# Moving operands of the FFN layers of a float32 block, moved to other byte offsets within 64

## What is computed

```python
D_MODEL, SEQ, D_FF = 1024, 256, 2816

def swiglu(x, w_gate, w_up, w_down):
    return (jax.nn.silu(x @ w_gate) * (x @ w_up)) @ w_down

# first block (c gives shifts, scales and gates g1, g2, g3)
h = h + 0.5 * g1 * swiglu(modulate(rmsnorm(h, norm_ff1), sh1, sc1), ...)   # FFN 0
h = h + g2 * token_mixing(modulate(rmsnorm(h, norm_mix), sh2, sc2), ...)   # mixer 0
h = h + 0.5 * g3 * swiglu(modulate(rmsnorm(h, norm_ff2), sh3, sc3), ...)   # FFN 1
h = rmsnorm(h, norm_final)
# second block
for l in range(2):
    x = x + 0.5 * swiglu_2(rms_norm(x, ffn1_norm[l]), ...)                 # FFN 2, 4
    x = x + mixers(rms_norm(x, mix_norm[l]) @ w_mix_in[l]) @ w_mix_out[l]  # mixers 1, 2
    x = x + 0.5 * swiglu_2(rms_norm(x, ffn2_norm[l]), ...)                 # FFN 3, 5
```

## Time and profile before

| what | us |
|---|---|
| median of 3 runs | 1628.17 |
| lowest, highest | 1627.67, 1628.93 |
| the profiled execution | 1633.48 |
| its span, first to last instruction | 1631.8 |
| TensorE with a matmul in flight | 1607.6 |
| VectorE busy | 1150.1 |
| ScalarE busy | 801.8 |

### The profile page before, as it was taken

The page is one execution under the profiler, slowest core; times in us unless marked ns, Lnnn a source line. Parts: engine busy times, 40 slices in busy tenths (PEclk is TensorE's granted clock), DMA queues, the critical chain, the costliest instruction groups (busy, mean ns, idle before and its releaser), DMA issues.

```text
span 1631.8 us, 33722 instructions
## 1 busy us (share of the span) xinstructions
PE 1607.6 (99%) x13569; PEld 1569.1 (96%) x13569; DVE 1150.1 (70%) x1470; ACT 801.8 (49%) x973; POOL 172.8 (11%) x193
## 2 busy tenths in 40 slices
PE   7999999999999999999999999999999999999999
PEld 4999998999999999999999999999999999999999
DVE  6877778878866657666688776656666588776653
ACT  3544445354544445444565654445444466564442
POOL 1100113700000000000043200000000025200000
PEclk9999998999999999999999999999999999999999
DMA  9998896755766477665754466558664764456653
GB/s 333 309 316 251 245 317 205 231 175 163 206 181 181 136 199 207 186 182 158 222 155 130 131 181 190 164 170 224 186 192 139 203 196 138 135 157 190 179 160 115
DMA packets 501553, 315.62 MB, mean 193 GB/s; under 512 B 14815, under 2 KB 489674, under 8 KB 501450
## 3 DMA queue, kind: packets, MB, share of 16 engines
q1 hardware_dynamic: 491824, 282.33, 60.7%
q0 software_dynamic: 8496, 29.92, 5.3%
q10 hardware_dynamic: 1130, 1.90, 0.3%
HBM read 313.04 MB, written 1.05 MB: 192 GB/s over the span
## 4 chain that ended last, share of the span: by engine, by line
PE 72%; DVE 3%; ACT 1%; issue 0%; ACTq 0%; DVEq 0%
PE accs L1755 20%; PE accs L1757 19%; PE accs L1756 19%; PE wide L1793 1%; PE accs L1793 1%; PE wide L1795 1%; PE accs L1795 1%; PE wide L1794 1%; PE accs L1794 1%; DVE wlo L1065 1%; PE wide L2026 1%; PE accs L1853 1%; PE accs L1854 1%; PE accs L1855 1%; PE bank L2097 0%
## 5 line engine op out<-in xcount | busy, mean ns | idle before, releaser
L1755 PE MATMUL accs<-uhi_room,whi 128*128 128x256 f32 x2304 | 650.8, 282 | 3.1 <-DVE ulo L1116 1.2
L1757 PE MATMUL accs<-uhi_room,wlo 128*128 128x256 f32 x2304 | 644.6, 280 | 0.0
L1756 PE MATMUL accs<-ulo,whi 128*128 128x256 f32 x2304 | 644.3, 280 | 0.0
L754 ACT CAST whi<-raw 128x2048 fp32r<-128x2048 f32 (+2 forms) x294 | 499.9, 1703 | 107.2 <-PE accs L1757 61.8
L1065 DVE TENSOR_TENSOR wlo<-raw,whi 128x2048 fp32r<-128x2048 f32 (+2 forms) x249 | 496.3, 2001 | 4.1 <-ACT gat L992 3.1
L1755 PEld LDWEIGHTS accs<-uhi_room,whi 128*128 128x128 f32 x2304 | 433.9, 188 | 11.5 <-issue 5.2
L1756 PEld LDWEIGHTS accs<-ulo,whi 128*128 128x128 f32 x2304 | 433.9, 188 | 1.2 <-issue 1.2
L1757 PEld LDWEIGHTS accs<-uhi_room,wlo 128*128 128x128 f32 x2304 | 433.7, 188 | 0.0
L1755 PE MATMUL accs<-hhi_room,whi 128*128 128x256 f32 x1056 | 297.0, 281 | 0.8 <-DVE wlo L1065 0.8
L1757 PE MATMUL accs<-hhi_room,wlo 128*128 128x256 f32 x1056 | 296.6, 281 | 0.0
L1756 PE MATMUL accs<-hlo_room,whi 128*128 128x256 f32 x1056 | 295.7, 280 | 0.0
(11 more groups left out here) (357 smaller groups left out, 2239.3 us busy)
## 6 DMA issues: line engine op xcount, KB each, us to landing
raw<-in_ffn_w_in SPq DMA_DIRECT2D x176, 512.0 KB, 5.0
in_turn<-in_w_ada POOLq DMA_DIRECT2D x56, 512.0 KB, 5.8
raw<-in_w_mix_in SPq DMA_DIRECT2D x52, 512.0 KB, 4.7
raw<-in_ffn_w_out SPq DMA_DIRECT2D x64, 384.0 KB, 3.6
raw<-in_w_ff_gate SPq DMA_DIRECT2D x44, 512.0 KB, 5.3
raw<-in_w_ff_up SPq DMA_DIRECT2D x44, 512.0 KB, 6.6
raw<-in_w_in SPq DMA_DIRECT2D x40, 512.0 KB, 4.9
raw<-in_ffn_w_out SPq DMA_DIRECT2D x64, 320.0 KB, 4.1
```

Source lines behind the costliest of these rows:

```text
L754: nc.scalar.copy(whi[:, n % RING, 0:cols], raw[:, n % RING, 0:cols]).then_inc(hi_ready, 1)
L1755: mm(dst, wh, xh, start=first, stop=False)
L1756: mm(dst, wh, xl, start=False, stop=False)
L1757: return mm(dst, wl, xh, start=False, stop=last)
```

## The change

`hhi` and `hlo` become lists with one view for each FFN, both at the same number of elements behind the start of their rooms, which now both start at offset 0; the rooms grow for it, and `hidden_end` too. `uhi` becomes a table `uhi_of` by the stage that reads it. Nothing else in the instructions changes: same shapes, same order, same waits.

| stage | moving operand | offset before | offset after |
|---|---|---|---|
| down projection of FFN 0, 1, 2, 3, 4, 5 | hhi, hlo | 32 | 28, 36, 20, 44, 4, 60 |
| up projection of FFN 2, 3, 4, 5 | u's high part | 32 | 28, 36, 20, 44 |
| the same | ulo | 32 | 32 |
| mixers 0, 1, 2; up projections of FFN 0, 1 | all | as above | the same |

```diff
+MIDDLE_FROM = [7, 9, 5, 11, 1, 15]
...
         uhi_room = sb("uhi_room", [P, KD * (T + 2)], F32R)
-        uhi = uhi_room[:, 0:KD * T].rearrange("p (k t) -> p k t", t=T)
+        def uhi_from(c):
+            return uhi_room[:, c:c + KD * T].rearrange("p (k t) -> p k t", t=T)
+
+        uhi = uhi_from(0)
         uhi_shift = uhi_room[:].rearrange("p (k t) -> p k t", t=T + 2)
-        uhi_shifted = uhi_shift[:, :, 0:T]
+        uhi_of = {"in0": uhi_shift[:, :, 0:T], "up1": uhi_shift[:, :, 0:T], "up2": uhi_from(15), "in1": uhi, "up3": uhi_from(1),
+                  "up4": uhi_from(13), "in2": uhi, "up5": uhi_from(3)}
...
-        hhi_room = hidden.enter_context(nc.sbuf_tensor("hhi_room", [P, ahead + KF * T], F32R))
-        hlo_room = hidden.enter_context(nc.sbuf_tensor("hlo_room", [P, KF * T], F32R))
-        hhi = hhi_room[:, ahead:].rearrange("p (k t) -> p k t", t=T)
-        hlo = hlo_room[:].rearrange("p (k t) -> p k t", t=T)
+        hhi_room = hidden.enter_context(nc.sbuf_tensor("hhi_room", [P, KF * T + 8 * ahead], F32R))
+        hlo_room = hidden.enter_context(nc.sbuf_tensor("hlo_room", [P, KF * T + 2 * ahead], F32R))
+        hhi, hlo = [[room[:, c:c + KF * T].rearrange("p (k t) -> p k t", t=T) for c in MIDDLE_FROM]
+                    for room in (hhi_room, hlo_room)]
...
-        sb("hidden_end", [P, 2 * KF])
+        sb("hidden_end", [P, 80])
...
-                            gained_hi(g, e0 + t // 2, t // 2, into=uhi if i else uhi_shifted)
+                            gained_hi(g, e0 + t // 2, t // 2, into=uhi_of[FOLLOWS[f"down{i}"]])
...
-                        ins = three(dst[:, j * T:(j + 1) * T], vh[:, k, c], vl[:, k, c], uhi[:, k], ulo[:, k],
+                        ins = three(dst[:, j * T:(j + 1) * T], vh[:, k, c], vl[:, k, c], xh[:, k], ulo[:, k],
                                     k == 0, k == kt - 1)
...
+                xh = uhi_of[f"up{i}"] if i else uhi
...
-                        ins = three(acc[(e0 + m) % 2][:, 0:T], vh[:, k], vl[:, k], hhi[:, kk], hlo[:, kk],
+                        ins = three(acc[(e0 + m) % 2][:, 0:T], vh[:, k], vl[:, k], hhi[i][:, kk], hlo[i][:, kk],
                                     kk == 0, kk == KF - 1)
```

More of the change, by code:

```diff
@@ L815, in step @@
                 def step(t, it=0):
-                    dst = tiles_of(hhi, t, it, RING)
+                    dst = tiles_of(hhi[i], t, it, RING)
                     if i == 0:
@@ L1010, in mixer @@
                     for k in (2 * t, 2 * t + 1):
-                        gained_hi(g, e0 + t, k, into=uhi if m else uhi_shifted)
+                        gained_hi(g, e0 + t, k, into=uhi_of[FOLLOWS[f"out{m}"]])
                     square_pair(["up1", "up3", "up5"][m], t)
@@ L1307, in step @@
                     src = hid[:, t % 2] if i == 0 else gate_up[:, t % 2, 1]
-                    nc.vector.tensor_tensor(tiles_of(hlo, t, it, RING), src, tiles_of(hhi, t, it, RING).bitcast(F32),
+                    nc.vector.tensor_tensor(tiles_of(hlo[i], t, it, RING), src, tiles_of(hhi[i], t, it, RING).bitcast(F32),
                                             ALU.subtract).then_inc(hlo_ready, 1)
@@ L1366, in down @@
                         if after is not None:
-                            gained_lo(SPLITS.index(FOLLOWS[f"down{i}"]), after, m, it, 2, uhi if i else uhi_shifted)
+                            gained_lo(SPLITS.index(FOLLOWS[f"down{i}"]), after, m, it, 2, uhi_of[FOLLOWS[f"down{i}"]])
                         split_ahead(n0 + t, it)
@@ L1690, in mixer @@
                     for k in (2 * t, 2 * t + 1):
-                        gained_lo(SPLITS.index(FOLLOWS[f"out{m}"]), next_gain(f"out{m}"), k, hi=uhi if m else uhi_shifted)
+                        gained_lo(SPLITS.index(FOLLOWS[f"out{m}"]), next_gain(f"out{m}"), k, hi=uhi_of[FOLLOWS[f"out{m}"]])
                     if t == 0 and m:
@@ L1763, in bank_free, with feature_tiles @@
                 pe.wait_ge(evacuated, it * per + e + 1)
-            def feature_tiles(n, dst, tiles, width, kt):
+            def feature_tiles(n, dst, tiles, width, kt, xh=uhi):
                 vh, vl = kview(whi, n % RING, KD, width), kview(wlo, n % RING, KD, width)
@@ L1770, in feature_tiles, with first_tiles @@
                     for k in range(kt):
-                        ins = three(dst[:, j * T:(j + 1) * T], vh[:, k, c], vl[:, k, c], uhi[:, k], ulo[:, k],
+                        ins = three(dst[:, j * T:(j + 1) * T], vh[:, k, c], vl[:, k, c], xh[:, k], ulo[:, k],
                                     k == 0, k == kt - 1)
                 return ins
-            def first_tiles(n, dst, waits, parted=(KD - 2, None)):
+            def first_tiles(n, dst, waits, parted=(KD - 2, None), xh=uhi):
                 at, between = parted
@@ L1940, in step @@
                     elif t == 0 and isinstance(it, int):
-                        ins = first_tiles(n0, acc[e0 % 2], waits, (4, second_part) if i == 0 else (KD - 2, None))
+                        ins = first_tiles(n0, acc[e0 % 2], waits, (4, second_part) if i == 0 else (KD - 2, None), xh)
                     elif i == 0 and t == 1 and isinstance(it, int):
@@ L1944, in step @@
                     else:
-                        ins = feature_tiles(n0 + t, acc[(e0 + t) % 2], range(2), 2 * P, KD)
+                        ins = feature_tiles(n0 + t, acc[(e0 + t) % 2], range(2), 2 * P, KD, xh)
                     ins.then_inc(chunk_used, 1)
```

## The result

The change makes the kernel slower: median 1645.3 us (1642.78 to 1645.61, 4 runs) against 1627.92 us (1625.63 to 1628.93, 4 runs), ratio 1.0107 with a 95% interval of 1.0095 to 1.0119, so +17.4 us. The forecast was slower by 5.0, at 1633.2; the time lies outside the range of 1623.5 to 1641.

A forecast was written before the change was run, and what follows sets the result against it. TensorE bounds the kernel: number of matmuls times the spacing of their starts. Up projections +3.4 us, down projections +1.6, upper half 0 make +5.0 on the median 1628.2: 1633.2 us, range 1623.5 to 1641.

The forecast's parts named there:

- Price of an offset in the lower half of 64 bytes: Streams at 28, 20, 4: up projections at 119.4 ns, +3.4 us; down projections at 118.6 ns, +1.6 us.
- 0 for the upper half: Stages at 36, 44, 60 keep their spacing: 0 us, bounds +3.5 and -0.6 us.
- The bound of 2.4 ns a matmul: Upper bound for low offsets, from FFN 1's up projection: 2.4 ns on each of 2992 matmuls, +7.2 us.
- The signs that were named: Spacings if right: up 2, 4 at 119+; down 0, 2, 4 at 118.4+; FFN 3, 5 at 116.7; down 1 at 117.8.
- the second rival: Every moving row starting off a 16-byte line costs 0.7 ns on 5984 matmuls, +4.2 us alone; chance 0.20.
- Token tiles as the price of a low offset in down projections: Mixer token tiles, streaming weights at offset 0, gave 118.6 ns for down projections of FFN 0, 2, 4: +1.6 us.
- The forecast's own interval, 1630.5 to 1638.9: Total time with lower half slow, upper half as before: 0 to +7.2 us and up to +3.5; chance 0.35.
- A constant offset costs nothing: FFN 1's 119.1 ns could come from offset changes between neighbours and 258 columns; 1628 us within 3; chance 0.27.
- Every start off 16 bytes costs: All six new offsets cross an extra 16-byte line: 0.7 ns on 5984 matmuls, 1632.4 us or 1637.4; chance 0.20.
- The change frees the slow stages: Stages at 117.8 ns in FFN 1, 2, 4 fall to 116.7: 4.1 us gained, 1624.1 us; chance 0.18.
- A doubling of the matmul at an offset of 4 behind a multiple of 8: Moving elements not fetched together: some 107 ns more on 5984 matmuls, +640 us; chance 0.03, outside the range.
- Two spacings at 32, chosen by something else: Identical code at 32 runs at 116.7 or 117.8 ns; in FFN 2 to 5 down projections share their up projection's spacing.

The follow-up runs named there:

- reversed: The changed kernel with the same offsets given to the FFNs in the other order, for the hidden layer and u's high part; 1643.35 us, ratio 1.0091.
- acts_up_64: Only the hidden layer at the new offsets, u back at 32, plus 64 bytes between weights and activations; 1654.75 us, ratio 1.0171.
- rooms_only: The changed kernel with its larger rooms but all offsets back at 32; 1627.48 us, ratio 0.9996.

## Why the prediction was wrong

- *The time is the number of matmuls times their spacing, no wait and no writer has a part.* Right: spacings account for 16.1 of 17.4 us.
- *"Price of an offset in the lower half of 64 bytes", and 0 for the upper half.* This step failed. The price was read from sums over four offsets each (0 to 24 against 32 to 56), and halves don't order it: 28, in the lower half, is free in a down projection (117.0 ns, forecast 118.6), while 36, in the upper, costs 3.4 ns (forecast 0). Of the six, those 4 bytes behind a multiple of 16 (4, 20, 36) are the dear ones and those 12 behind (28, 44, 60) the cheap ones, and reversed repeats this in other FFNs. The rows of FFN 1's up projection couldn't show it: their offsets are all multiples of 8, each has neighbours at other offsets, and none of the six new ones is among them.
- *The bound of 2.4 ns a matmul* was no bound: offset 4 costs 5.5, 20 costs 4.4. Low offsets came to +9.6 us (28, 20 and 4: -0.1 + 1.4 + 2.3 + 3.1 + 2.9) for 5.0 forecast and 7.2 at most, high ones to +6.5 (1.8 + 2.5 + 0.5 + 1.2 + 0.5) for 0 and 3.5 at most. Both ends were taken from offsets that the change doesn't use.
- *The signs that were named.* The up projections of FFN 2 and 4 passed the mark of 119 (119.0 and 120.7), the second by more than forecast, and the down projections of FFN 2 and 4 the mark of 118.4. FFN 0's down projection did not (117.0), FFN 1's did not stay at 117.8 (121.1), and FFN 3 and 5 left 116.7 for 117.7 to 119.0. The last is the sign given for the second rival, whose price of 0.7 ns for every start off 16 bytes is nonetheless wrong: the stages differ by -0.2 to +5.5 ns. That the kernel got slower came out; that it did so through the lower half is right for 9.6 us of the 16.1, and at no price of a half.
- *Token tiles as the price of a low offset in down projections.* They stream at offset 0 but with the roles exchanged, so their place against the stationary tensor is another one. The price taken from them, 118.6 ns (seven threes; the mean of all is 118.2), did not carry over: a down projection at 0 has 120.0, and those at 28, 20 and 4 have 117.0, 122.2 and 123.3. In acts_up_64 the token tiles went from 118.2 to 117.7 ns while the stages at 32 went up to 120.0.
- *The forecast's own interval, 1630.5 to 1638.9.* Its lower end doesn't follow from the bounds given: with 0 from both halves it is 1628.2. The range of 1623.5 to 1641 doesn't use it.
- *A constant offset costs nothing*: out, by every down projection at 4, 20, 36. *Every start off 16 bytes costs*: in down projections 28 costs nothing (-0.2 ns) and 44 and 60 no more than the step from 116.7 to 117.8 that 32 shows by itself, and 0, 16 and 48, which lie on such a line, cost more than these. *The change frees the slow stages*: in no stage but FFN 0's down projection (-0.2 ns). *A doubling of the matmul at an offset of 4 behind a multiple of 8*: out, no spacing is above 123.8 ns.
- *Two spacings at 32, chosen by something else.* Right, and there is a third, 120.0 ns. That a down projection has the spacing of the up projection ahead of it is chance: in rooms_only FFN 2 has 117.7 and 116.7. rooms_only and the kernel before differ by 1 ns in some stages and by nothing in the median.

Shown: each of the two parts costs half; in this layout the offset orders the price of a down projection whatever the FFN; the end or the length of the row has a part; moving activations against the tensors ahead of them changes nearly every stage, moving all together none beyond the rhythms of 32; and the spacing of the down projections looked at is the same with ScalarE, VectorE and GpSimd idle or at work. Argued only: that it is the weight load under way during a matmul that the moving rows meet. It is the one user of the tensors ahead that is left in the idle stretches, but no run changes it alone. Open: the rule that gives 116.7 or 123.3 ns from the addresses, its period (128 bytes is not one), and what picks among the rhythms at 32. A direct test would move the slots of the weights alone, in steps; it wasn't tried.

## What to carry to other kernels

Where TensorE streams without waits, count starts in long windows and compare stages: a few ns a matmul hardly show in the busy share (99 and 98%) or in the durations (0.28 and 0.29 us), and are worth 1% here. Byte placement of the moving rows against the weights is a real lever (from 1627 to 1655 us here), but it has to be scanned on the chip with the offsets that are to be used. Here the place before the change was already as good as any tried. And whoever enlarges or inserts a tensor between weights and activations changes it for every stage behind; a pad that restores the distance should undo it, which was not tried. Don't read a price from rows whose neighbours differ in the same property.

## What had not been expected of the hardware

The spacing of 256-column matmuls moves in steps, most of which hold for a whole stage: at 2.4 GHz 116.7, 117.8 and 120.0 ns at one and the same offset, and up to 123.8 ns at others. With 252 columns it goes down to 113.4 ns. Some stages change step midway with nothing changed in the code: FFN 0's up projection before runs at 116.7 ns for five eighths of its matmuls and ends at 117.8, and FFN 5's down projection in acts_up_64 falls from 119.9 to 117.9. A pad of 64 bytes between weights and activations alone took the stages at 32 from 116.7 or 117.8 to 120.0 ns, 19 us on the kernel; the same pad ahead of both left the kernel at 1634.04 us (1635.96 without it).
